# The 17 small parameter loads move from ScalarE's DMA queue to GpSimd's, and the constants are split

## The reference

```
aq, ak, av, bq, bk, bv, bgate, bbeta, ba = split_last(x @ w_in, EVEN_SPLITS)
...
qkv = jax.nn.silu(causal_depthwise_conv(jnp.concatenate([bq, bk, bv], axis=-1), conv_w))
beta = jax.nn.sigmoid(bbeta.astype(f32))
g = -jnp.exp(a_log.astype(f32)) * jax.nn.softplus(ba.astype(f32) + dt_bias)
```

## Time and profile before

| | us |
|---|---|
| median of three runs | 1794.38 |
| the three runs | 1786.88, 1794.38, 1794.71 |
| span of the profiled execution, first to last instruction | 1787.8 |
| PE busy | 1635.9 (92%) |
| DVE busy | 1301.3 (73%) |
| ACT busy | 982.0 (55%) |
| POOL busy | 24.2 (1%) |

### The profile page before, as it was taken

One profiled execution on the slowest core, in us unless ns is written; L12 is line 12 of the kernel. 1 busy time (PEld: TensorE's weight loads), 2 busy tenths in 40 slices (PEclk: granted clock), 3 DMA queues, 4 the chain that ended last, 5 costly groups with the idle time before them and its releaser, 6 DMA issues.

```text
span 1787.8 us, 22866 instructions
## 1 busy us (share of the span) xinstructions
PE 1635.9 (92%) x8767; PEld 1380.9 (77%) x8768; DVE 1301.3 (73%) x1096; ACT 982.0 (55%) x816; POOL 24.2 (1%) x17
## 2 busy tenths in 40 slices
PE   3978989997998869899999999999999999999996
PEld 3868669996998757788788787787787887887884
DVE  2757365456576575788788788888887887887896
ACT  2333134442334443577676676676676776775772
POOL 1000000000100000000000000000000000000000
PEclk7989989998999989899999999999999999999998
DMA  8150045555453014699799899899899898998991
GB/s 265 48 212 1 31 158 187 181 179 158 142 167 140 1 47 171 248 365 368 269 372 356 291 370 350 294 365 344 298 364 340 316 362 307 346 369 286 347 380 58
DMA packets 214792, 440.41 MB, mean 246 GB/s; under 512 B 11292, under 2 KB 61780, under 8 KB 214740
## 3 DMA queue, kind: packets, MB, share of 16 engines
q1 hardware_dynamic: 208496, 433.96, 68.2%
q10 hardware_dynamic: 6244, 5.73, 1.0%
HBM read 438.61 MB, written 1.05 MB: 246 GB/s over the span
## 4 chain that ended last, share of the span: by engine, by line
PE 81%; DVE 9%; ACT 5%; issue 2%; ACTq 1%; POOL 0%; POOLq 0%; DVEq 0%
PE ps L1876 16%; PE ps L1878 16%; PE ps L1877 16%; PE ps L1429 5%; PE ps L1430 5%; PE ps L1431 5%; ACT w_hi L780 2%; DVE w_lo L1262 2%; PE ps L1941 2%; PE ps L1422 2%; PE ps L1864 1%; DVE w_lo L889 1%; PE ps L1688 1%; PE ps L1689 1%; PE ps L1690 1%
## 5 line engine op out<-in xcount | busy, mean ns | idle before, releaser
L1262 DVE TENSOR_TENSOR w_lo<-raw,w_hi 128x2048 fp32r<-128x2048 f32 x336 | 767.0, 2291 | 145.3 <-ACT w_hi L780 144.2
L780 ACT CAST w_hi<-raw 128x2048 fp32r<-128x2048 f32 x336 | 642.0, 1913 | 206.7 <-PE ps L1878 192.3
L1876 PE MATMUL ps<-w_hi,xg_hi 128*128 128x512 f32 x896 | 356.4, 398 | 3.5 <-DVE w_lo L1262 2.0
L1878 PE MATMUL ps<-w_hi,xg_lo 128*128 128x512 f32 x896 | 349.8, 390 | 0.0
L1877 PE MATMUL ps<-w_lo,xg_hi 128*128 128x512 f32 x896 | 348.9, 389 | 0.0
L889 DVE TENSOR_TENSOR w_lo<-raw,w_hi 128x2048 fp32r<-128x2048 f32 (+1 forms) x73 | 168.3, 2312 | 133.4 <-ACT w_hi L575 133.3
L1429 PE MATMUL ps<-xT_hi,w_hi 128*128 128x256 f32 x768 | 221.5, 288 | 27.3 <-DVE w_lo L889 22.1
L1430 PE MATMUL ps<-xT_lo,w_hi 128*128 128x256 f32 x768 | 220.5, 287 | 0.0
L1431 PE MATMUL ps<-xT_hi,w_lo 128*128 128x256 f32 x768 | 220.5, 287 | 0.0
L575 ACT CAST w_hi<-raw 128x2048 fp32r<-128x2048 f32 (+1 forms) x73 | 136.3, 1877 | 146.5 <-PE ps L1431 99.8
L1876 PEld LDWEIGHTS ps<-w_hi,xg_hi 128*128 128x128 f32 x896 | 168.3, 188 | 41.1 <-issue 4.5
(11 more groups left out here) (332 smaller groups left out, 1575.7 us busy)
## 6 DMA issues: line engine op xcount, KB each, us to landing
raw<-in_moe_w_gate SPq DMA_DIRECT2D x112, 1024.0 KB, 7.1
raw<-in_moe_w_up SPq DMA_DIRECT2D x112, 1024.0 KB, 7.4
raw<-in_moe_w_down SPq DMA_DIRECT2D x112, 1024.0 KB, 6.9
raw<-in_ssm_w_in SPq DMA_DIRECT2D x20, 1024.0 KB, 5.4
raw<-in_ffn_w_gate SPq DMA_DIRECT2D x11, 1024.0 KB, 5.3
raw<-in_ffn_w_up SPq DMA_DIRECT2D x11, 1024.0 KB, 5.3
raw<-in_ffn_w_down SPq DMA_DIRECT2D x11, 1024.0 KB, 5.0
raw<-in_even_w_in SPq DMA_DIRECT2D x10, 1024.0 KB, 11.9
```

The lines of the kernel that those rows point to most:

```text
L780: act.copy(w_hi[:, n % CUT, :], raw[:, i, :]).then_inc(sem("hi_made"), 1)
L1262: TTO(w_lo[:, n % CUT, :], raw[:, n % RAW, :], w_hi[:, n % CUT, :].bitcast(F32), ALU.subtract).then_inc(lo_made, 1)
L1876: mm(out_ap, hi, whi, start=start, stop=False)
L1878: return mm(out_ap, lo, whi, start=False, stop=stop)
```

## The change

ACT's 17 small loads go to POOL. POOL first waits for the identity and x (`x_loaded`, 32), issues 11 of them, waits until DVE has made `w_lo` of piece 2, issues the other six, and then goes on with `join` and the rest. SP loads the identity (the first 128 columns of `const`) first, then x, then pieces 0 to 5, and behind them the other 1576 columns of `const` and the rows of the first LayerNorm. Those three loads count on `ln_loaded`, whose thresholds rise by 16, and two waits on it are new: one on DVE ahead of the rotary step, one on PE ahead of the first product that reads `tri`.

```diff
         @block.sync
         def _(sp):
+            sp.dma_start(const[:, 0:P], dram["shape_consts"][:, 0:P]).then_inc(sem("x_loaded"), 16)
             sp.dma_start(x_tok[:, :, :], dram["x"][0].rearrange("(t p) d -> p t d", p=P)).then_inc(sem("x_loaded"), 16)
-            sp.dma_start(const[:, :], dram["shape_consts"]).then_inc(sem("x_loaded"), 16)
...
             for n in range(N0):
                 piece(n, n % RAW_D, pieces0[n])
+                if n == RAW_D - 1:
+                    sp.dma_start(const[:, P:C_W], dram["shape_consts"][:, P:C_W]).then_inc(sem("ln_loaded"), 16)
+                    sp.dma_start(ln_gb[:, 0], dram["ln_g"][0][0].partition_broadcast(P)).then_inc(sem("ln_loaded"), 16)
+                    sp.dma_start(ln_gb[:, 1], dram["ln_b"][0][0].partition_broadcast(P)).then_inc(sem("ln_loaded"), 16)
...
             pool.wait_ge(sem("pool_set"), 3)
-            def join(n):
...
-        @block.scalar
-        def _(act):
+
             def small(dst, src, loaded_="params_loaded"):
-                act.dma_start(dst, src).then_inc(sem(loaded_), 16)
+                pool.dma_start(dst, src).then_inc(sem(loaded_), 16)
...
+            pool.wait_ge(sem("x_loaded"), 32)
             small(prow_b[0:CONV * NDN, :], dram["dn_conv_w"][0].rearrange("k (j p) -> (k j) p", p=P), "taps_loaded")
...
             small(dn_nw[:, :], row("dn_norm_w", 0))
+            pool.wait_ge(d_lo_made, RAW_D + CUT)
             small(w_dt[:, :, :], cols(w_in1, SI + NXBC * P, SH))
...
             small(brt[:, :], row("moe_b_router", 0))
 
+            def join(n):
...
+        @block.scalar
+        def _(act):
...
-            load_ln(0)
 
             act.wait_ge(sem("params_loaded"), 16 * 13)
...
-                dve.wait_ge(sem("ln_loaded"), 32 * (n + 1))
+                dve.wait_ge(sem("ln_loaded"), 32 * (n + 1) + 16)
...
+            dve.wait_ge(sem("ln_loaded"), 16 * 3)
             dve.wait_ge(sem("q_copied"), TT)
...
             pe.wait_ge(sem("dn_gb"), 1)
+            pe.wait_ge(sem("ln_loaded"), 16 * 3)
```

More of the change, by code:

```diff
@@ L508, in _, with small, row @@
             pool.wait_ge(sem("pool_set"), 3)
+            def small(dst, src, loaded_="params_loaded"):
+                pool.dma_start(dst, src).then_inc(sem(loaded_), 16)
+            def row(name, *idx):
+                a = dram[name]
+                for i in idx:
+                    a = a[i]
+                return a.partition_broadcast(P)
+            pool.wait_ge(sem("x_loaded"), 32)
+            small(prow_b[0:CONV * NDN, :], dram["dn_conv_w"][0].rearrange("k (j p) -> (k j) p", p=P), "taps_loaded")
+            small(prow_b[CONV * NDN:CONV * NDN + NX, :], dram["ssm_norm_w"][0].rearrange("(j p) -> j p", p=P), "taps_loaded")
+            small(prow_b[CONV * NDN + NX:CONV * NDN + NX + NXBC, :], dram["ssm_conv_b"][0].rearrange("(j p) -> j p", p=P), "taps_loaded")
+            small(prow_a[0:CONV * NXBC, :], dram["ssm_conv_w"][0].rearrange("k (j p) -> (k j) p", p=P), "taps_loaded")
+            small(w_ba[:, :, :], cols(w_in0, BA0, 2 * DH))
+            small(identb[:, :], dram["shape_consts_b"][:, 0:P])
+            small(maskb[:, :], dram["shape_consts_b"][:, P:2 * P])
+            small(sinks[:, :], row("swa_sinks", 0))
+            small(dn_al[:, :], row("dn_a_log", 0))
+            small(dn_dtb[:, :], row("dn_dt_bias", 0))
+            small(dn_nw[:, :], row("dn_norm_w", 0))
+            pool.wait_ge(d_lo_made, RAW_D + CUT)
+            small(w_dt[:, :, :], cols(w_in1, SI + NXBC * P, SH))
+            small(ssm_al[:, :], row("ssm_a_log", 0))
+            small(ssm_dtb[:, :], row("ssm_dt_bias", 0))
+            small(ssm_db[:, :], row("ssm_d", 0))
+            small(w_rt[:, :, :], cols(dram["moe_w_router"][0], 0, E))
+            small(brt[:, :], row("moe_b_router", 0))
             def join(n):
@@ L527, in _ @@
         def _(act):
-            def small(dst, src, loaded_="params_loaded"):
-                act.dma_start(dst, src).then_inc(sem(loaded_), 16)
[L531 to L553, removed]
             def load_ln(n):
-                if n:
-                    act.wait_ge(sem("ln_done"), TT * n)
+                act.wait_ge(sem("ln_done"), TT * n)
                 act.dma_start(ln_gb[:, 0], dram["ln_g"][n // 2][n % 2].partition_broadcast(P)).then_inc(sem("ln_loaded"), 16)
@@ L685, in _ @@
                 load_ln(1)
-                act.wait_ge(sem("ln_loaded"), 64)
+                act.wait_ge(sem("ln_loaded"), 80)
                 return
@@ L711, in _ @@
                 load_ln(2)
-                act.wait_ge(sem("ln_loaded"), 96)
+                act.wait_ge(sem("ln_loaded"), 112)
                 return
@@ L791, in _ @@
             if limit < 5:
-                act.wait_ge(sem("ln_loaded"), 128)
+                act.wait_ge(sem("ln_loaded"), 144)
                 return
```

## The result

| | before | after |
|---|---|---|
| median | 1793.69 us (6 runs, 1786.88 to 1795.28) | 1780.24 us (6 runs, 1773.99 to 1783.90) |
| ratio, 95% interval | | 0.9929 [0.9912, 0.9946] |
| span of the profiled execution | 1787.8 | 1781.9 |
| its time | | 1783.66 |
| three `w_lo` end, PE's first product | 35.38, 31.12 | 21.08, 15.21 |

The changed kernel is faster by 12.7 us (9.7 to 15.8), which is 0.0071 of 1793.69.

What follows compares the result with a forecast made beforehand. The prediction took ACT's DMA issues until 19.65 us as delaying the first stage, then DVE's wait for 13 small loads as its gate. Span 1787.8 less 7.9 gave 1779.9; plus 6.6, median 1786.5 us, range 1776 to 1795.

Steps and rivals of the forecast that it cites:

- x, transposes, ACT freed: At the kernel's start: x at 6.5 us, PE's first product at 14.8 instead of 31.12, 16.3 us earlier.
- What PE alone would allow, 28.6: DVE's tap copy `pcol`: at 28.6 instead of 44.89 us if DVE waited only for PE's turned taps.
- `join` under DVE's wait: POOL's `join` runs from 26.7 to 31.2 us while DVE waits, at no cost; otherwise up to 4.5 us.
- POOL issues at 1.11 us each: POOL's small loads, at ACT's average issue time: 11 issues end at 18.7 us, the other six at 26.7.
- The last of the six lands at 37: Last six small loads: 2560 packets taking turns with SP's land at 37.4 us, so DVE goes on at 37, 7.9 earlier.
- the first rival: Small loads at the first stage arrive by 28.6 us, full 16.3 us gained: 1778.1; chance 0.22.
- The sum: Whole kernel: profiled span 1787.8 less 7.9 gives 1779.9; with 6.6 from span to median, 1786.5 us.
- the likeliest case's own: Whole kernel: range 1780 to 1792 us if DVE's wait before the taps ends between 31 and 41.9; chance 0.55.
- rival 1: DVE's wait before the taps: parameters come in time, PE's transposes end it at 28.6 us; 1778.1; chance 0.22.
- Rival 2: POOL's issuing bounds the first stage: gain 1.7 us (1792.7) or a loss (1806); chance 0.20.
- The rest of `const`, pieces 6 and 7, PE's fallen clock: hidden: First stage: `const` in by 30 us, pieces 5.4 later, PE some 2 us at half speed; none costs time.
- The time is gained here and given back later: Behind the first stage: a load that sets a later stage takes the gain back, about 1794 us; chance 0.03.

Runs made afterwards that it cites:

- the kernel without the middle wait: Changed kernel minus POOL's wait for `w_lo` of piece 2, so all 17 loads issue in a row: 1772.89 us, ratio 0.9888; repeated, 1775.57, ratio 0.9926.
- without waits: Changed kernel minus both POOL waits, for x and for `w_lo` of piece 2, with `join` straight behind the loads: 1781.16 us.
- the moved gate: Changed kernel with DVE's wait for the 13 loads moved from before the tap copy to before the rotary step, with two `ssm_db` copies: 1776.40 us, ratio 0.9924.

## Why the prediction was right, and where its size was off

1. **x, transposes, ACT freed.** x at 6.65 for 6.5; ACT's table load ends at 2.02; PE's first product at 15.21 for 14.8. Right. Piece 2 came at 16.86 instead of 15.8 and `w_lo` 2 ended at 21.1 instead of 20.0. The byte count itself was nearly right: SP's queue had moved 4.25 MB, all up to piece 2, at 15.5 for the 15.1 forecast. The rest is that the piece landed 1.4 us after its bytes by this count and not 0.7; why was not tried.
2. **What PE alone would allow, 28.6.** Right: 28.54 to 29.19 in the kernels in which nothing else was waited for and `join` lay clear of the first `w_lo`.
3. **`join` under DVE's wait.** Right, from 25.39 to 30.02; the kernel before with `join` late shows it worth 3.9 us.
4. **POOL issues at 1.11 us each.** Too dear: 0.54 for most, 0.9 for the wide ones. It mattered little: the last issue ended at 25.3 instead of 26.7. Nor did DVE's subtraction hold POOL's issues up, for which the text had no row: they took 0.54 beside it.
5. **The last of the six lands at 37.** This is the term that was mis-sized: 33.2. The count of 2560 packets, one for each run, holds on ACT's queue (41.7 with the six there) and not on POOL's (208 packets). The text had weighed that: with the Trainium skill's rule of 9 to 17 descriptors to a packet (DMA: Bandwidth & Descriptors, Queues, rings and completion order) it gave the first rival's time, and the 12.3 runs per packet agree with this rule on POOL's queue. But the rule didn't bring the rival's time either. What neither had is the 3 to 4.5 us ahead of a queue's first packet: on POOL's queue the six moved their first packet at 25.92, and even with SP's queue held back a load took 4.4 us from issue to landing. 24.74 + 4.4 + 4.1 = 33.2. So the forecast came within 4 us of `pcol` partly by luck: twelve times too many packets made it late, and a delay that it put at nothing made it early. (A slip of its own adds 1 us: from 20.5 to 24.5 its rate lets 71 small packets pass and not 60, which would give 36.4. The 60 fit only a start at 21.1.)
6. **The sum.** Stage gain 11.6 for 7.9; measured at the end 12.7 (9.7 to 15.8). 1780.24 lies within the range and at the lower edge of the likeliest case's own. The 6.6 us that the sum adds from span to median are no property of the kernel: after the change the median is 1.7 below the profiled span. Against the span the forecast was 1779.9 for 1781.9, 3.7 too little gained in the stage and 5.5 given back behind it, which it had not foreseen. The mechanism was that of the forecast, a wait for a DMA that takes the place of the one removed; rival 1's mechanism, PE ending the wait, is that of the kernel without the middle wait. Rival 2, POOL's issuing as the bound, is out: a mean of 0.6 us, not above 2.0.
7. **The rest of `const`, pieces 6 and 7, PE's fallen clock: hidden.** Right in this stage: the granted clock is 0.60 from 36 to 38 us and 0.54 from 38 to 40 after PE's rest, nearer 4 us at half speed than the 2 forecast, and the chain passes it by over DVE and ACT. "The time is gained here and given back later" had 0.03, for a load that sets a later stage. In the profiled pair 2.4 us are given back before the first LayerNorm, in a stretch where the granted clock is lower (0.88 for 0.91); the cause stays open.

What is shown of the 11.6 us: 3.9 from `join` (added alone to the kernel before) and 0.5 to 1.2 from the split (taken alone from the changed one, about what two profiles of one kernel differ by). The rest, some 7, is left by subtraction for ACT, which no longer issues ahead of its copies; with the 17 loads back on ACT all of the gain is gone. The middle wait left 4.1 more on the table.

## What to carry to other kernels

When a wait covers a list of loads, it is as late as the last one issued, whatever that one is for: look up the name of the DMA that ends the wait, and either issue it with the others or move the wait to its first reader. A rule about packets that is read from one engine's DMA queue need not hold for another's, so bound the new queue apart, its time ahead of the first packet too. And an elementwise operation on GpSimd belongs where VectorE waits: moving one such instruction was a third of this gain.

## What the hardware showed that was not expected

- **ACT's issuing and POOL's.** 17 loads held ACT for 18.9 us; the same loads take POOL 6.4 us for eleven and 3.9 for six. An issue of 128 runs takes 0.54 beside a DVE subtraction that runs at its usual 2.25 us (they start at 12.54 and 12.77 in the timeline).
- **POOL and DVE.** Where `join` lay over `w_lo` for 3.4 us (without the middle wait), 3.6 (without waits) and 0.9 (the moved gate), DVE's work took 3.3, 3.5 and 0.8 longer: DVE stood nearly as long as POOL's elementwise sum ran beside it.
- **Time ahead of the first packet.** On POOL's queue it was 3.28 us from issue to first packet with SP held back, and 4.07 to 4.67 beside SP's traffic. On ACT's queue it was 1.13 and 2.06 us at the very start of two kernels (the one with the 17 loads back on ACT, and the one before), and 3.72 and 3.94 for the six loads beside SP's traffic.
- **The clock's record can miss a slow stretch.** PE's first products after the change, and the stretch of 15 to 20 us with its granted clock (1.00):

```profile
15.78 0.41 PE L1437 MATMUL ps<-xT_hi,w_lo 128*128 128x256 f32 x1
15.99 0.41 PE L1435 MATMUL ps<-xT_hi,w_hi 128*128 128x256 f32 x1
...
19.50 0.28 PE L1437 MATMUL ps<-xT_hi,w_lo 128*128 128x256 f32 x1
19.62 0.28 PE L1435 MATMUL ps<-xT_hi,w_hi 128*128 128x256 f32 x1
```

```profile
15.00:20.00 5.00, 4.79 (x25) 4.82 (x26) 3.48 (x3) 1.90 (x1) 0.00 (x0) 1.00 1.03 330
```

  Products follow each other at 0.21 us until 19.2 and at 0.12 from then on, 4.0 us after PE's start, as the prediction had it from the earlier trace rows, but the record reads 1.00 throughout. Where the two differ, read the spacing of the products.
- **The expert stage comes in steps of 3.1 us**: POOL's wait over it is 1068.1 to 1068.4 in seven profiles, 1071.3 to 1071.5 in six, 1074.6 in one. The changed kernel has one profile in each of the first two groups. A gain below 3 us can't be read from a single pair of spans here.
